# Sample attention of a hybrid decoder step: scores and values of 16 sample rows in four column groups of 24 rows in place of three of 32

## The reference

```
x = x + 1/2 * SwiGLU_1(RMSNorm(x))
z = RMSNorm(x) @ w_in        (pooling | attention q,k,v | retention q,k,v,gate)
  A: causal pooling, 4 groups of 64
  B: 6 heads of 64, block-sparse attention: blocks of 256 keys, the best 3 past blocks and the own one, ALiBi
  C: 6 heads of 64, retention, RMS-normalised per head, gated
x = x + concat(A, B, C) @ w_out
x = x + 1/2 * SwiGLU_2(RMSNorm(x))
```

## Time and profile before

| | |
|---|---|
| median of 3 runs | 1356.29 us (1355.41 to 1356.34) |
| profiled execution, its own time | 1353.38 us |
| its span | 1351.7 us |
| TensorE matmul busy | 1322.9 us, 98% |
| VectorE, ScalarE, GpSimd busy | 57%, 49%, 17% |
| granted TensorE clock, mean | 0.996 |
| moved by DMA | 235.27 MB, mean 174 GB/s |

### The profile page before, as it was taken

How to read it: one execution, slowest core, us unless ns; L and a number is a source line. 1 busy time by engine, 2 the same in 40 slices (tenths; PEclk the granted TensorE clock), 3 DMA queues, 4 the chain that set the end, 5 groups by cost and what they waited for, 6 DMA issues and landing times.

```text
span 1351.7 us, 28355 instructions
## 1 busy us (share of the span) xinstructions
PE 1322.9 (98%) x11129; PEld 1276.1 (94%) x11129; DVE 772.7 (57%) x842; ACT 657.3 (49%) x741; POOL 233.4 (17%) x342
## 2 busy tenths in 40 slices
PE   6999999999999999999999999999999999999998
PEld 5999999999878999999999999999997799999998
DVE  5555555666556655554555555565755565555444
ACT  5555543434444655553355555333443555555434
POOL 4000000356440100000101000013755120000001
PEclk9999999999999999999999999999999999999998
DMA  6655544769787444444446654447797854444443
GB/s 198 206 175 163 167 141 157 191 184 228 184 279 224 143 155 155 142 134 157 158 130 193 186 177 134 156 147 208 182 243 223 255 173 156 140 150 155 141 144 128
DMA packets 213487, 235.27 MB, mean 174 GB/s; under 512 B 15006, under 2 KB 207272, under 8 KB 213396
## 3 DMA queue, kind: packets, MB, share of 16 engines
q1 hardware_dynamic: 205436, 211.19, 51.2%
q0 software_dynamic: 7840, 22.85, 6.0%
q10 hardware_dynamic: 120, 0.03, 0.0%
HBM read 228.83 MB, written 5.32 MB: 173 GB/s over the span
## 4 chain that ended last, share of the span: by engine, by line
PE 92%; issue 5%; DMA 1%; DVE 1%; POOLq 1%; SPq 0%; POOL 0%; ACT 0%; DVEq 0%; ACTq 0%
PE ps L1303 22%; PE ps L1304 22%; PE ps L1305 22%; PE ps L1390 4%; PE ps L1392 4%; PE ps L1391 4%; PE ps L1536 3%; PE ps L1573 2%; PE ps L1710 1%; PE ps L1712 1%; PE ps L1711 1%; PE ps L1431 1%; PE ps L1488 1%; DMA x_tok<-in_x_sample 0%; PE ps L1524 0%
## 5 line engine op out<-in xcount | busy, mean ns | idle before, releaser
L649 ACT ACTIVATE w_hi<-w_raw 128x2048 fp32r<-128x2048 f32 x170 | 325.4, 1914 | 538.6 <-PE ps L1305 421.0
L922 DVE TENSOR_TENSOR w_lo<-w_raw,w_hi 128x2048 fp32r<-128x2048 f32 x162 | 371.9, 2295 | 187.5 <-ACT w_hi L649 185.3
L1303 PE MATMUL ps<-h_hi,w_hi 128*128 128x320 f32 x768 | 239.4, 312 | 4.0 <-DVE x L989 2.3
L1305 PE MATMUL ps<-h_hi,w_lo 128*128 128x320 f32 x768 | 238.3, 310 | 0.0
L1304 PE MATMUL ps<-h_lo,w_hi 128*128 128x320 f32 x768 | 238.2, 310 | 0.0
L1303 PE MATMUL ps<-g_hi,w_hi 128*128 128x320 f32 x704 | 218.0, 310 | 0.0
L1305 PE MATMUL ps<-g_hi,w_lo 128*128 128x320 f32 x704 | 217.5, 309 | 0.0
L1304 PE MATMUL ps<-g_lo,w_hi 128*128 128x320 f32 x704 | 217.5, 309 | 0.0
L1303 PE MATMUL ps<-act_hi,w_hi 128*128 128x320 f32 x704 | 217.4, 309 | 0.0
L1304 PE MATMUL ps<-act_lo,w_hi 128*128 128x320 f32 x704 | 217.4, 309 | 0.0
L1305 PE MATMUL ps<-act_hi,w_lo 128*128 128x320 f32 x704 | 217.4, 309 | 0.0
(11 more groups left out here) (286 smaller groups left out, 1770.7 us busy)
## 6 DMA issues: line engine op xcount, KB each, us to landing
w_raw<-in_ffn_w_in SPq DMA_DIRECT2D x90, 1024.0 KB, 5.1
w_raw<-in_ffn_w_out SPq DMA_DIRECT2D x32, 896.0 KB, 4.6
w_raw<-in_w_in SPq DMA_DIRECT2D x22, 1024.0 KB, 6.0
kbuf<-in_cache_k SPq DMA_DIRECT2D x96, 192.0 KB, 4.9
w_raw<-in_ffn_w_out SPq DMA_DIRECT2D x16, 1024.0 KB, 5.0
kbuf<-in_cache_v SPq DMA_DIRECT2D x64, 192.0 KB, 3.9
w_raw<-in_w_out SPq DMA_DIRECT2D x8, 1024.0 KB, 6.6
kbuf<-in_cache_k POOLq DMA_DIRECT2D x32, 192.0 KB, 3.5
```

The costliest lines, as they stand in the source:

```text
L649: act.activation(w_hi[:, slot, :], w_raw[:, slot, :], ACT.Copy).then_inc(hi_done, 1)
L922: dve.tensor_tensor(w_lo[:, slot, :], w_raw[:, slot, :], w_hi[:, slot, :].bitcast(F32), ALU.subtract).then_inc(split_done, 1)
L1303: pe.matmul(out, w_hi[:, slot, w], hi[:, k, :], start=(k == 0), stop=False)
L1305: ins = pe.matmul(out, w_lo[:, slot, w], hi[:, k, :], start=False, stop=(k == k_all - 1))
```

## The change

Rows of the scores are laid out as sequence, group of three heads, head, query: four column groups g of 24 rows (in 32), so that g // 2 is the sequence and g % 2 the half of the heads. The constants, tiles and waits follow:

- `key_scores(p)` is one loop of 6 steps x 4 column groups x 4 row groups; it needs all four turns of the pair, and counts `sc_done` once. `own_scores(p)` has 8 matmuls and waits for `qb_ok`. `qprep` writes `q_sc` first, then `q_bd` in six copies.
- All tiles of scores have 128 partitions. `transpose_probs` makes nine transposes of 128 x 128 into three banks; `probs_evac` picks 24 of every 32 columns.
- `smp_out(p)` does both sequences of a pair, four column groups on 192 value columns. A V place `E` is new, and the order of places differs. `out_evac(p)` and `transpose_out(p)` follow; the latter is six f32 matmuls with a picked identity.
- `mean_squares` is called for two tiles and later for the third.
- The lists of TensorE, ScalarE, VectorE, GpSimd and SP are reordered in the last part of the stage.

```diff
-        V_HOME = "XWBACDBA"
+        V_HOME = "XWBACEDB"
...
-            return part if p else (2, 6)[part]
-
-        def out_bank(p, bb):
-
-            return (6 if p else 4) + bb
+            return ((2, 6, 3), (2, 3, 5), (0, 1, 5), (0, 1, 4))[p][part]
+
+        def out_bank(p):
+
+            return (4, 6, 7, 6)[p]
...
                 def next_k(p, bb):
 
-                    wait_apart(sp_e, sc_done, L * NB + (1 if p == 1 else p * 2 + (bb - 1)))
+                    wait_apart(sp_e, sc_done, L * (NB // 2) + p)
...
+                wait_apart(sp_e, sc_done, (NB // 2) * L + 4)
                 for u in range(2, 4):
-                    wait_apart(sp_e, sc_done, NB * L + u + 5)
                     load_v(u)
+                wait_apart(sp_e, pv_done, (NB // 2) * L + 1)
                 for slot, cols in enumerate((slice(0, 256), slice(256, 512))):
-                    wait_apart(sp_e, pv_done, NB * L + 1 + slot)
                     square(A["w_out"], L, half0 + C_WO // 2, cols, slot, apart=True)
-                wait_apart(sp_e, pv_done, NB * L + 3)
-                load_v(6)
-                wait_apart(sp_e, pv_done, NB * L + 4)
+                wait_apart(sp_e, pv_done, (NB // 2) * L + 2)
                 load_v(7)
...
                 load_v_all(4)
-                for h in range(2, H):
-                    spread_v(h)
+                spread_v(2)
+                spread_v(3)
+                wait_apart(pool, r_done, H * L + H)
+                load_v_all(5)
+                spread_v(4)
+                spread_v(5)
                 wait_apart(pool, vbd_used, H * L + H)
                 wait_apart(pool, pt2_done, NB * L + 4)
-                load_v_all(5)
+                load_v_all(6)
...
                     act.wait_ge(pt2_done, L * 8 + p * 2 + 1)
-                    act.activation(pt[:, 0:480], ps[:, t_bank(p, 0), 0:480], ACT.Copy).then_inc(pt2_evac, 1)
+                    act.activation(to(every, 0, 384), used(every, 0, 0), ACT.Copy).then_inc(pt2_evac, 1)
...
                 ret_square(1)
-                out_evac(0, 0)
-                out_evac(0, 1)
+                probs_evac(1)
+                out_evac(0)
                 ret_square(2)
                 act.wait_ge(sp_done, L + 1)
                 act.activation(sp_new[:], ps[:, 6, 320:512].rearrange("p (f v) -> p f v", f=3), ACT.Copy).then_inc(st_prm, 1)
-                probs_evac(1)
-                for f in range(3):
-                    root_o(f)
-                out_evac(1, 0)
+                root_o(0)
+                root_o(1)
                 probs_evac(2)
+                root_o(2)
+                mix_hi(12)
+                or_high(0)
+                or_high(1)
+                exps(3)
+                out_evac(1)
                 y_high(0)
-                exps(3)
-                out_evac(1, 1)
-                mix_hi(12)
-                out_evac(2, 0)
+                or_high(2)
+                out_evac(2)
                 probs_evac(3)
-                for f in range(3):
-                    or_high(f)
                 y_high(1)
...
+                turn_k(1, 1, 0)
                 mix_lo(6)
-                turn_k(1, 1, 0)
+                turn_k(1, 1, 1)
...
                 gate(1)
+                soft_bias(3)
                 new_state(1)
                 gate(2)
-                new_state(2)
-                soft_bias(3)
...
                 or_norm(0)
-                y_rest(0)
+                new_state(2)
                 or_norm(1)
                 or_norm(2)
                 dve.drain()
                 mix_lo(12)
+                or_lo(0)
+                or_lo(1)
                 soft_sum(3)
+                y_rest(0)
+                or_lo(2)
                 y_rest(1)
-                for f in range(3):
-                    or_lo(f)
...
+                def key_scores(p):
+
+                    wait_apart(pe, kt_ok, L * 16 + p * 4 + 4)
+                    for n in range(6):
+                        slot, j = divmod(n, 2)
+                        for g in range(4):
+                            c = (3 * (g % 2) + slot) * HD + 32 * j
+                            at_q = 192 * g + 64 * slot + 32 * j
                             for r in range(4):
                                 R = slice(32 * r, 32 * r + 32)
-                                ins = pe.matmul(ps[32 * f:32 * f + 32, 2 + r, 0:256], q_sc[p][R, bb, f, a, j, :],
-                                                kbuf[k_home(p, bb)][R, :, c:c + 32], start=(bb == 0 and n == 0), stop=(bb == 1 and n == 3))
+                                ins = pe.matmul(ps[32 * g:32 * g + 32, 2 + r, 0:256], q_sc[p][R, at_q:at_q + 32],
+                                                kbuf[k_home(p, g // 2)][R, :, c:c + 32], start=(n == 0), stop=(n == 5))
                     ins.then_inc(sc_done, 1)
...
+                def smp_out(p):
+
+
+                    pe.wait_ge(pt2_evac, L * 8 + p * 2 + 2)
+                    if p == 3:
+                        pe.wait_ge(o_evac, L * 4 + 2)
+                    for u in (2 * p, 2 * p + 1):
+                        pe.wait_ge(v_landed[V_HOME[u]], v_count(L, u))
                     for j in range(PAGES + 1):
-                        for f in range(3):
+                        for g in range(4):
                             rows = P if j < PAGES else SMP
-                            c = 96 * (2 * (j % 4) + j // 4 if j < PAGES else j) + 32 * f
-                            cols = slice(P * f, P * f + P)
-                            v = v_page(u, j, cols) if j < PAGES else v_own[:, cols]
-                            ins = pe.matmul(ps[32 * f:32 * f + 32, out_bank(p, bb), 0:P], pt_s[p % 2][0:rows, c:c + 32], v,
+                            at_j = 2 * (j % 4) + j // 4 if j < PAGES else j
+                            n = 32 if g < 3 or at_j < 7 else 24
+                            c = 96 * at_j + 24 * g
+                            cols = slice(192 * (g % 2), 192 * (g % 2) + 192)
+                            v = v_page(2 * p + g // 2, j, cols) if j < PAGES else v_own[:, cols]
+                            ins = pe.matmul(ps[32 * g:32 * g + n, out_bank(p), 0:192], pt_s[p % 2][0:rows, c:c + n], v,
                                             start=(j == 0), stop=(j == PAGES))
                     ins.then_inc(pv_done, 1)
...
-                    for bb in range(2):
-                        wait_apart(pe, o_evac, L * NB + p * 2 + (bb + 1))
-                        ins = pe.transpose(ps[:, 5 if p < 3 else 1, 96 * bb:96 * bb + 96], o_tok[p % 2][:, bb, :], ident[0:96, 0:96])
+                    wait_apart(pe, o_evac, L * 4 + p + 1)
+                    rows = ident[:].rearrange("p (b g s q) -> p b g s q", b=2, g=2, s=4)
+                    for h in range(H):
+                        f, r, _ = head(h)
+                        out = ps[r, 5 if p < 3 else 1, 16 * f:16 * f + 16].rearrange("p (b q) -> p b q", b=2)
+                        ins = pe.matmul(out, o_tok[p % 2][:, HD * (h % 3):HD * (h % 3) + HD], rows[:, :, h // 3, h % 3, :],
+                                        start=True, stop=True)
...
                 ret_out(1)
                 wait_apart(pe, sm_in, L * 4 + 4)
-                smp_out(0, 0)
+                transpose_probs(1)
+                smp_out(0)
                 smp_state(1)
-                smp_out(0, 1)
                 ret_out(2)
+                wait_apart(pe, pt2_evac, L * 8 + 4)
+                mean_squares((0, 1))
                 wait_apart(pe, r_mask, H * L + 6)
-                transpose_probs(1)
+                transpose_probs(2)
                 smp_state(2)
-                mean_squares()
+                wait_apart(pe, o_evac, L * 4 + 1)
+                mean_squares((2,))
                 wait_apart(pe, st_prm, L + 1)
-                smp_out(1, 0)
-                transpose_probs(2)
+                smp_out(1)
+                wait_apart(pe, pt2_evac, L * 8 + 6)
                 transpose_out(0)
-                wait_apart(pe, st_smp, 3 * L + 3)
-                smp_out(1, 1)
...
-                smp_out(2, 0)
+                wait_apart(pe, st_smp, 3 * L + 3)
+                smp_out(2)
+                wait_apart(pe, o_std, 3 * L + 3)
                 transpose_probs(3)
                 wait_apart(pe, ys_low, 4 * L + 1)
                 transpose_out(1)
-                smp_out(2, 1)
-                smp_out(3, 0)
                 chunk_split(half0 + C_WO // 2, 0)
                 pe.wait_ge(att_low, L + 1)
-                pe.wait_ge(ret_low, 3 * L + 3)
                 out_part(0, (0, 1), early, True)
                 wait_apart(pe, ys_low, 4 * L + 2)
                 transpose_out(2)
-                smp_out(3, 1)
+                smp_out(3)
                 chunk_split(half0 + C_WO // 2, 1)
+                pe.wait_ge(pt2_evac, L * 8 + 8)
+                out_part(1, (0,), early[:2], True)
                 wait_apart(pe, ys_low, 4 * L + 3)
-                out_part(1, (0,), early[:2], True)
```

(30 more changed lines are left out.)

127 lines of the change are left out of this document (57 added, 70 removed).

## The result

The changed kernel takes 1357.9 us (median of 12 runs) where the kernel before takes 1353.6 on the same chips: a ratio of 1.0033 (95% interval 1.0020 to 1.0046). It is slower, by 0.33%; the prediction had it faster by 0.3%. The profiled execution took 1359.9 us, with a span of 1358.3.

A forecast was written before the change was run, and what follows sets the result against it. The prediction took TensorE, busy 98% of the span, to bound the kernel. Its terms, -10.0 + 1.9 + 2.9 + 0.4 - 1.0 - 2.9 + 4.4 = -4.3, took 1356.3 us to 1352.0; range 1347.0 to 1355.5.

The forecast's parts named there:

- Where the first three pairs' saving goes: Key scores, first three pairs: later key loads make TensorE wait before the third pair, cancelling the faster passes: 0 us.
- The fourth pair: Key scores of the fourth pair: VectorE waits for no keys there, so 0.5 us a layer is saved, -1.0 in all.
- Clock, 0 forecast: TensorE's low stretch before the dense part grows, but one clock loss of 1.5 us stays as now: 0.
- The rival "both layers": Rival: the granted clock falls before the dense part in both layers, giving 1353.5 us; chance 0.13.
- Waits that come, +4.4: Last part of stage: TensorE waits 0.9 us for the fourth pair's exponentials and 1.3 for y_rest, in each layer.
- the rival to which I gave 0.08: Rival: w_out lands late, exponentials stand behind it, each microsecond past +4.7 stops TensorE one per layer; 1360 at 4 late.
- Values: Probabilities times values: four column groups overlap like three, so a pair takes 3.2 us in place of 4.46: -10.0 us.
- Waits for values gone: TensorE's waits for values behind the fourth pair's transposes go, as values are asked for earlier or needed later: -2.9 us.
- Output transposes: Two transposes per pair become six f32 matmuls, 0.54 us a pair: +2.9 us over both layers.
- Transposes of the probabilities: Nine transposes go from 96 rows to 128 x 128, 0.026 us more each, eight pairs: +1.9 us.
- Key scores near 17 ns a pass: Sign of being right: sixteen tiles bring 192 passes from 22 ns to near 17 each, 1.0 us saved a pair.
- Keys in time: Rival: the loads' start doesn't limit key landing, so three pairs keep 1.0 + 0.5 + 0.5 us a layer: 1348.0; chance 0.17.

The follow-up runs named there:

- run 7: Changed kernel, w_hi/w_lo later, old retention state asked for later; first kernel also has second pair's key turns back (1.0002 to kernel before), second not (0.9977).
- the tile-order run: Changed kernel with the sixteen key-score tiles of a round visited with the four column groups innermost, the four row groups outside; one run, 1369 us.

## Why the prediction was wrong

**The step that failed** is "Where the first three pairs' saving goes", the 0 for three pairs. Measured from the first pair to the third pair's own scores they lose 2.9 us in layer one and 5.2 in layer two. The prediction saw the mechanism (one release a pair, VectorE behind the landing, TensorE waiting for the turn), but it had the loads of keys and the last turn 1.4 us late, paid for by the stall that goes and the faster passes, and the pair ending where it had ended before. The loads were 3.5 and 3.4 us late in the two layers, the last turns 3.9 and 5.3. Layer one, forecast and measured: second pair starts at 305.0, 306.85; loads 310.3, 312.42; last turn ends 338.0, 340.5; pair 4.6 us long, 5.5; third pair ends 342.6, 346.1. Of the 1.8 us at the second pair, 0.7 is the first pair's saving (0.27 us where I took 1.0), 0.6 is a shift that was there before the pairs, and 0.5 is a gap that the profile calls issue. The rest of the pair's length is the clock. Over both layers the 8.0 us are about 7.2 of waits for the turn, 3.8 of clock and 1.0 of gaps, less 2.6 of stalls that went and 1.7 of faster passes. What the terms of the sum treated as free is TensorE arriving first and waiting: from there on what delays the last turn delays TensorE. How far late loads delay that turn depends on what else is in the queues (run 7).

The fourth pair came out at -1.35 in layer one (no stall left) and +0.2 in layer two (a stall of 1.79), against -0.5 each: the sum is right by luck.

**Clock, 0 forecast.** I asked whether it falls before the dense part and not whether it falls behind the wait that I had just put in front of the third pair. The stretch at 1.2 GHz is 1.5 us of loss in the third pair of layer one (5.46 less 3.95), 2.3 in layer two, and one more 1.7 before layer two's dense part. The rival "both layers" was right about the last of these. A section of the Trainium skill (TensorE: Matmul & The Clock Gate, HAM oscillation — how this bites in real kernels) describes matmul bursts that start at the lower clock because a wait for data stands before each. The trace agrees: 0.50 at each of the four waits of 2.5 to 3.6 us, and 1.00 at the same place in the runs where that wait is gone. But the waits don't settle it alone: in run 7's first kernel the same wait of 2.08 us has 0.50 behind it in layer one and 1.00 in layer two, and in its second kernel's trace stalls of 3.02 and 2.95 us have 1.00 behind them.

**Waits that come, +4.4.** Measured 5.0 for the exponentials and 0.1 for y_rest, 5.1. The forecast's own terms (0.9 and 1.3) are near what the run without the sixth unit's values shows (1.1 and 1.4). In the changed kernel w_out lands late, the rival to which I gave 0.08, and the exponentials wait for it, which I had named as a sign of being wrong. But the rival's price was wrong: each microsecond does not stop TensorE for one. Of the 1.6 us more a layer at the exponentials y_rest gives 1.2 back, and the two waits sum to 2.5 us with w_out in time too.

**What held.** Values: 72 passes a pair take 3.19 us in all eight pairs (3.2). Waits for values gone. Output transposes 0.46 each (0.54), mean squares +0.2. Transposes of the probabilities +0.29 in the mean of the eight, for +0.24. The last part of the stage as a whole: -3.1 for -3.3. The rows of the table leave out 1.1 us that the forecast has in its terms (the first pair's transposes of probabilities, the last pair's of the output), so the same terms make -2.0, and among them is a clock loss of 1.7 in layer two that the forecast had at 0.

**Key scores near 17 ns a pass** were wrong: 19. Steady starts are 17 ns apart, but each round of 32 passes holds one pause (158 ns with 256 columns, 43 with 128), which I had not priced.

**Keys in time** would not have brought 1348.0 either: when the keys were early on sixteen tiles, a stall of 3.0 us took their place.

What stays open: the gap of 0.5 us before the second pair (0.3 to 0.5 in the kernels of the new layout, whatever the order of the turns, except where a longer wait or stall takes its place); and why the clock also fell where no long wait preceded it (below).

## What to carry to other kernels

When two releases are merged into one, price the work that waits for the *start* of the next transfer: follow release, request, landing, conversion and consumer in us, and if the consumer arrives first at the end of that chain, a later landing is paid in full, and the clock may be paid on top. A load that an in-order engine must convert belongs behind everything that the critical engine needs from that engine, and moving one such item only moves the wait to the next one. Before saving passes in a stretch, look whether that stretch stalls for its own instructions: there a faster rate buys little.

## What the runs showed of the hardware

Instruction supply. In the fourteen traces TensorE stalls 61 times within a pair of key scores, for 0.1 to 3.3 us, and each time it resumes 2.2 to 2.8 us after the one 16 KB packet of queue 8 (instructions) starts. So the stall is long where that packet comes late. Transfers of the run with the state later, 336.0 to 339.5 us and then 339.5 to 342.3 (packets, MB, share of the 16 engines):
```profile
q1 hardware_dynamic: 1069, 1.17, 108.4%
```
```profile
q1 hardware_dynamic: 1114, 0.64, 74.9%
q8 instruction: 1, 0.02, 2.4%
q14 instruction: 1, 0.01, 1.2%
```
No instruction packet moves in the first 3.5 us, with 334 GB/s of data; the two come behind it, queue 8's at 339.89, and TensorE resumes at 342.31. In the seventh experiment's first run the stall reached 3.3 us. More traffic does not always mean a longer stall: in the kernel before, the third pair stalls 1.96 us in layer one, with 231 GB/s from 336.0 to 339.5, and 0.60 in layer two, with 337 GB/s from 996.0 to 998.2. The Trainium skill (Runtime: NRT & Kernel Launch, Instruction fetch mechanics) has fetching hidden by the pace of issue; these rows contradict it for bursts of short passes. What delays the packet, the data ahead of it or something else, no run varied alone.

Small passes on many tiles. On 32-row tiles with 256 columns 192 passes start in 4.9 to 5.5 us on eight tiles at a time (25 to 29 ns each), 3.91 on twelve (20 ns) and 3.64 on sixteen (19 ns): from twelve to sixteen almost nothing is won.

The clock. In the tile-order run it stood at 1.2 GHz for 23 us with TensorE busy throughout, in a stretch that is the changed kernel's:
```profile
1040.00:1063.00 23.00, 23.00 (x119) 15.01 (x112) 10.08 (x36) 6.38 (x10) 10.57 (x17) 0.50 0.71 227
```
No run shows why; that run's time (one, 1369 us) is therefore not compared.
